# FFN1's last group beside keys and values of blocks 0 to 2, norm products on GpSimd, conditioning columns as dots on VectorE

## What is computed

```python
mod = (silu(c) @ w_ada + b_ada)             # 9 rows of 1024: sh1 sc1 gt1 sh2 sc2 gt2 sh3 sc3 gt3
h = rms_norm(x) * (1 + sc1) + sh1
x = x + 0.5 * gt1 * swiglu(h)               # FFN1, hidden width 2816
h = rms_norm(x) * (1 + sc2) + sh2
x = x + gt2 * (sig(gA) * P_A(chunk band attention) + sig(gB) * P_B(multi-scale pool)) @ w_o
h = rms_norm(x) * (1 + sc3) + sh3
x = x + 0.5 * gt3 * swiglu(h)               # FFN2
```

## Time and profile before

| what | value |
|---|---|
| median of 3 runs | 1545.3 us (1543.4 to 1545.4) |
| the profiled execution | 1544.8 us, its slowest core's span 1543.2 us |
| spans of the 8 cores | 1537.7 to 1543.2 us |
| mean granted TensorE clock | 0.989 to 1.000 |
| bytes moved by DMA on that core | 107.13 MB, mean 69 GB/s |

### The profile page before, as it was taken

How to read it: one execution, slowest core, us unless ns; L and a number is a source line. 1 busy time by engine, 2 the same in 40 slices (tenths; PEclk the granted TensorE clock), 3 DMA queues, 4 the chain that set the end, 5 groups by cost and what they waited for, 6 DMA issues and landing times.

```text
span 1543.2 us, 23259 instructions; the slowest of 8 cores (1537.7 to 1543.2 us)
## 1 busy us (share of the span) xinstructions
PE 1486.7 (96%) x8336; PEld 703.2 (46%) x8336; DVE 815.5 (53%) x1290; ACT 451.3 (29%) x630; POOL 119.4 (8%) x170
## 2 busy tenths in 40 slices
PE   2899999999999999999999999999999999999998
PEld 1344444444444444454564454444444444444443
DVE  2366344172272756678765568746453616162644
ACT  3470111101101036468855453523401010101010
POOL 1100100100001012200000000203000000000000
PEclk9999999999999999999999999999999999999999
DMA  9951433513515211430044363347132221211022
GB/s 204 243 102 28 76 69 55 99 25 69 96 28 102 48 41 38 123 60 15 1 93 86 56 130 63 69 82 116 28 55 53 44 42 16 47 28 28 1 110 109
DMA packets 24303, 107.13 MB, mean 69 GB/s; under 512 B 2816, under 2 KB 3072, under 8 KB 21760
## 3 DMA queue, kind: packets, MB, share of 16 engines
q0 software_dynamic: 21312, 75.67, 29.0%
q1 hardware_dynamic: 2880, 29.98, 5.6%
HBM read 168.71 MB, written 12.58 MB: 117 GB/s over the span
## 4 chain that ended last, share of the span: by engine, by line
PE 91%; DMA 3%; DVE 3%; issue 2%; ACT 1%; POOL 0%; DVEq 0%; ACTq 0%; POOLq 0%
PE ps L714 44%; PE ps L742 21%; PE ps L1081 7%; PE ps L887 4%; PE ps L1113 4%; PE ps L1094 3%; DMA arena<-w_ada 3%; PE ps L1027 2%; DVE arena L513 1%; PE ps L933 1%; PE ps L969 1%; PE ps L870 1%; DVE arena L519 1%; PE ps L563 1%; PE ps L609 1%
## 5 line engine op out<-in xcount | busy, mean ns | idle before, releaser
L714 PE MATMUL ps<-arena 128*128 128x512 bf16 x3152 | 694.4, 381 | 4.4 <-DVE arena L519 4.0
L507 ACT ACTIVATE arena<-ps 128x512 bf16<-128x512 f32 (+3 forms) x426 | 268.5, 652 | 946.3 <-PE ps L714 790.4
L714 PEld LDWEIGHTS ps<-arena 128*128 128x128 bf16 x3152 | 307.8, 98 | 376.3 <-issue 16.2
L519 DVE SCALAR_TENSOR_TENSOR arena<-ps,arena 128x512 f32<-128x512 f32 (+1 forms) x500 | 360.4, 748 | 73.6 <-ACT arena L507 22.6
L513 DVE TENSOR_TENSOR arena<-arena,ps 128x512 bf16<-128x512 bf16 x198 | 135.1, 687 | 486.8 <-PE ps L714 476.1
L742 PE MATMUL ps<-arena 128*128 128x512 bf16 x1584 | 345.0, 379 | 1.3 <-DVE arena L513 1.2
L742 PEld LDWEIGHTS ps<-arena 128*128 128x128 bf16 x1584 | 154.4, 98 | 188.3 <-issue 5.5
L513 DVE TENSOR_TENSOR arena<-arena 128x1024 f32<-128x1024 f32 (+8 forms) x228 | 173.6, 780 | 33.8 <-ACT arena L507 27.6
L1081 PE MATMUL ps<-arena 128*128 128x512 bf16 x512 | 116.3, 379 | 1.4 <-ACT arena L507 1.0
L507 ACT ACTIVATE arena<-arena 128x512 f32<-128x512 f32 (+2 forms) x86 | 89.3, 1053 | 35.2 <-DVE arena L519 20.8
L1081 PEld LDWEIGHTS ps<-arena 128*128 128x128 bf16 x512 | 49.1, 98 | 59.8 <-issue 2.4
(11 more groups left out here) (65 smaller groups left out, 516.6 us busy)
## 6 DMA issues: line engine op xcount, KB each, us to landing
arena<-w_ada POOLq DMA_DIRECT2D x36, 512.0 KB, 8.8
arena<-w_gate POOLq DMA_DIRECT2D x24, 512.0 KB, 8.5
arena<-w1i POOLq DMA_DIRECT2D x22, 512.0 KB, 6.5
arena<-w3i POOLq DMA_DIRECT2D x22, 512.0 KB, 5.3
arena<-x SPq DMA_DIRECT2D x5, 2048.0 KB, 15.5
outT<-arena SPq DMA_DIRECT2D x8, 1024.0 KB, 3.9
arena<-w1o POOLq DMA_DIRECT2D x10, 512.0 KB, 6.8
arena<-w_kqvu POOLq DMA_DIRECT2D x10, 512.0 KB, 7.6
```

The costliest lines, as they stand in the source:

```text
L507: return e.activation(out=o, in_=i, func=func, scale=scale)
L519: return e.scalar_tensor_tensor(out=out, in0=in0() if callable(in0) else in0, scalar=scalar, in1=in1() if callable(in1) else in1, op0=op0, ...
L714: ins = e.matmul(pst(t), lhsT=w[:, kt, :], rhs=hk(b, kt), start=(kt == 0), stop=(kt == 7))
```

## The change

- The last 24 chunks of `w_ada` become 48 dots: `ada_dot` loads 128 rows of the transposed matrix (512 KB, f32, on SyncE's queue) into one of two buffers in `EXPB`'s place and has VectorE multiply them by silu(c) (broadcast to all partitions, `CCB`) with a running sum. They follow three of four units from unit 23 on. A single addition of all 48 biases and the `der` rows come after the last.
- The last group of FFN1 keeps its activations in `ACTL` (block 0 to 2 in the place of the keys of the same block, 3 and 4 in the halo's), the SiLU outputs of blocks 2 to 4 in `SAL`, and its weights in a ring "l" outside of the mixer's slots but one; the group before uses five slots ("p"). Units and outputs of its blocks 2, 3 and 4 get ramps f2, f3 and f4, and all ramps are new. `outp` now has the gate row among the reads of its matrix products.
- The four products of the second and the third norm go to GpSimd; the planner's costs of some operations are changed.
- The bias table comes in four parts into two buffers, not in two into one.
- The last block's stores are split in 4, 2, 1 and 1 tiles, not in 4 and 4.

```diff
@@ -19,11 +19,12 @@
 SILU, EXP, LN, TANH = "silu", "exp", "ln", "tanh"
-RAMPS = {"v0a": (6.86, 12.16), "k0a": (10.15, 11.87), "k0b": (10.76, 11.77), "v0b": (12.6, 12.7),
-         "a0": (10.39, 12.64), "u0": (10.68, 12.89), "k3": (11.4, 12.42), "k4": (11.01, 14.15),
-         "v3": (15.11, 15.16), "v4": (13.29, 13.34), "q4": (13.4, 13.6), "a1": (14.08, 16.3),
-         "g0": (13.99, 15.41), "o0": (17.33, 18.34), "u1": (15.09, 18.95), "g1": (19.52, 20.02),
-         "n1": (16.9, 20.3), "o1": (21.22, 21.31)}
+RAMPS = {"f2": (-2.27, 2.35), "f3": (3.2, 4.57), "f4": (1.96, 11.57), "v0a": (10.79, 16.74),
+         "k0a": (13.06, 13.07), "k0b": (11.58, 11.63), "v0b": (12.47, 16.3), "a0": (3.81, 9.54),
+         "u0": (9.96, 17.67), "k3": (14.97, 15.02), "k4": (11.18, 25.82), "v3": (14.62, 16.19),
+         "v4": (25.19, 33.87), "q4": (11.34, 12.92), "a1": (13.34, 16.32), "g0": (13.27, 15.92),
+         "o0": (9.88, 25.49), "u1": (10.59, 20.44), "g1": (14.47, 25.98), "n1": (18.69, 26.76),
+         "o1": (26.57, 27.85)}
@@ -381,7 +382,9 @@
     cst_d = din("cst", [128, NCST])
-    ada_d = din("w_ada", [36, 128, 2048])
+    ada_d = din("w_ada", [12, 128, 2048])
+    adat_d = din("w_adat", [48, 128, 1024])
+    crow_d = din("crow", [128, 1024])
@@ -450,7 +453,9 @@
     o_w = alloc(6 * 4096)
-    TABT = view(o_mrg, F32, (4 * TABW,))
+    ACTL = [view(o, BF16, (4, TB)) for o in (o_kt, o_kt + 4096, o_kt + 8192, o_mrg, o_mrg + 4096)]
+    SAL = [view(o_mrg + 8192 + 1024 * i, BF16, (TB,)) for i in range(3)]
+    TABT = [view(o, F32, (2 * TABW,)) for o in (o_mrg + 11264, o_x + 2 * 16384 + 8192)]
@@ -475,6 +480,8 @@
              "g": [o_qt, o_qt + 4096, o_expb + 4096, o_att, o_att + 4096] + [o_w + 4096 * i for i in range(6)],
+             "p": [o_w + 4096 * i for i in range(5)],
+             "l": [o_expb, o_expb + 4096, o_att, o_att + 4096, o_qt + 4096, o_w + 5 * 4096],
@@ -533,6 +540,9 @@
         return H[:, b, kt, :]
+    def ramp(t0, t1, n):
+        return lambda i: t0 + (t1 - t0) * (i + 0.5) / n
@@ -584,6 +594,17 @@
+    ADS = [view(o_expb + 4096 * i, F32, (1024,)) for i in range(2)]
+    CCB = view(o_kq, BF16, (1024,))
+
+    def ada_dot(j, deps=()):
+        wt = ADS[j % 2]
+        S.op("sp", lambda e: e.dma_start(out=wt, in_=adat_d[j - 24]), writes=[wt], dma="d_ads%d" % (j % 2), nbytes=1 << 19,
+             deps=deps)
+        S.op("dve", lambda e: e.scalar_tensor_tensor(out=wt, in0=wt, scalar=1.0, in1=CCB, op0=ALU.mult, op1=ALU.mult,
+                                                     accum_out=MOD[:, j:j + 1]),
+             reads=[wt, CCB], writes=[wt, MOD[:, j:j + 1]], cost=1.22)
+
@@ -622,7 +643,10 @@
             rb = bass.AP(rs.tensor, rs.offset, [list(rs.ap[0]), [0, 2], [1, TB]])
-            tt(tb, xp, rb, ALU.mult, [xp, rs], [tb], 1.1)
+            if sub > 0:
+                tt(tb, xp, rb, ALU.mult, [xp, rs], [tb], 2.3, eng="pool")
+            else:
+                tt(tb, xp, rb, ALU.mult, [xp, rs], [tb], 1.22)
@@ -631,7 +655,7 @@
                         out=hk(b, kt), in0=ti, scalar1=s1, scalar2=s2, op0=ALU.mult, op1=ALU.add),
-                        reads=[ti, sc, sh], writes=[hk(b, kt)], cost=0.49)
+                        reads=[ti, sc, sh], writes=[hk(b, kt)], cost=0.6)
@@ -689,11 +713,14 @@
     def ffn(wi_d, wo_dd, sub, blocks, first):
-        ada_next = [12] if first else [36]
+        ada_next = [24] if first else [72]
...
-        def unit(jl, b, wt):
+        def hid(jl, b, last):
+            return ACTL[b][:, jl, :] if last and first else ACTB[:, jl, b, :]
+
+        def unit(jl, b, wt, last=False):
@@ -714,24 +741,29 @@
                     S.op("pe", mm, reads=[wt, H[:, b, :, :]], writes=[t], cost=mmc(8, 512), also=[tb] if t is ta else (), stream="ab")
-            sa = SA[sa_pos[0] % 3]
+            sa = (SAL if last and first and b >= 2 else SA)[sa_pos[0] % 3]
...
             act(sa, lambda: pst(ta), AF.Silu, reads=[ta], writes=[sa], cost=0.6, tset=SILU)
-            tt(ACTB[:, jl, b, :], sa, lambda: pst(tb), ALU.mult, [sa, tb], [ACTB[:, jl, b, :]], 0.69)
+            hd = hid(jl, b, last)
+            tt(hd, sa, lambda: pst(tb), ALU.mult, [sa, tb], [hd], 0.69)
...
             n = ucount[0]
-            if ada_next[0] < 36 and n > 20 and n % 3 == 0:
-                c = ada_next[0]
-                ada_load(c, [uops[max(0, n - 7)]])
-                t = Tile()
-                ada_mm(c, t, c)
-                ada_out(t, c, 1)
+            if ada_next[0] < 72 and n > 22 and n % 4 != 0:
+                j = ada_next[0]
+                if j == 24:
+                    S.op("sp", lambda e: e.dma_start(out=ADS[1], in_=crow_d), writes=[ADS[1]], dma="d_ads1", nbytes=1 << 19,
+                         deps=[uops[10]])
+                    act(CCB, ADS[1], AF.Silu, reads=[ADS[1]], writes=[CCB], cost=1.0, tset=SILU)
+                ada_dot(j, [uops[max(0, n - 4)]])
                 ada_next[0] += 1
-                if ada_next[0] == 36:
+                if ada_next[0] == 72:
+                    lo, hi = 24, 72
+                    tt(MOD[:, lo:hi], MOD[:, lo:hi], CST[:, 8 + lo:8 + hi], ALU.add, [MOD[:, lo:hi], CST], [MOD[:, lo:hi]], 0.17)
...
-        def outp(b, nk, wos):
+        def outp(b, nk, wos, last=False):
+            hd = [hid(jl, b, last) for jl in range(nk)]
@@ -739,10 +771,10 @@
                         c0 = (jl % 2) * 1024 + n * 128
-                        ins = e.matmul(pst(t), lhsT=wos[jl // 2][:, c0:c0 + 128], rhs=ACTB[:, jl, b, :],
+                        ins = e.matmul(pst(t), lhsT=wos[jl // 2][:, c0:c0 + 128], rhs=hd[jl],
...
                     return ins
-                S.op("pe", mm, reads=[w for w in wos] + [ACTB[:, jl, b, :] for jl in range(nk)], writes=[t],
+                S.op("pe", mm, reads=[w for w in wos] + hd + [DER[:, 3 * sub + 2, :]], writes=[t],
@@ -752,7 +784,7 @@
             nk = GSIZES[g]
-            ring = "g" if not first else ("s" if g == 0 else "f")
+            ring = "g" if not first else ("s" if g == 0 else "l" if g == ng - 1 else "p" if g == ng - 2 else "f")
@@ -791,22 +823,27 @@
                             norm(blocks[i + 1], 0)
+                    pf = ramp(*RAMPS["f%d" % b], nk + 2) if lastg and first and b >= 2 else None
                     for jl in range(nk):
-                        unit(jl, b, wts[jl])
+                        if pf:
+                            S.prio = pf(jl)
+                        unit(jl, b, wts[jl], lastg)
                     if lastg:
-                        outp(b, nk, wos)
+                        if pf:
+                            S.prio = pf(nk + 1)
+                        outp(b, nk, wos, lastg)
                         if first:
-                            S.prio = 0.0 if b <= 2 else 9.0
+                            S.prio = 0.0 if b <= 2 else 10.5
...
                         if not first:
-                            for n in range(0, 8, 4):
-                                S.op("sp", lambda e, n=n, b=b: e.dma_start(out=outT[b - 1][:, n:n + 4, :],
-                                                                           in_=XB[:, b - 1, n:n + 4, :]),
-                                     reads=[XB[:, b - 1, n:n + 4, :]], dma="d_st", nbytes=1 << 20,
+                            for n, w in ((0, 4), (4, 2), (6, 1), (7, 1)) if b == blocks[-1] else ((0, 4), (4, 4)):
+                                S.op("sp", lambda e, n=n, w=w, b=b: e.dma_start(out=outT[b - 1][:, n:n + w, :],
+                                                                                in_=XB[:, b - 1, n:n + w, :]),
+                                     reads=[XB[:, b - 1, n:n + w, :]], dma="d_st", nbytes=w << 18,
@@ -841,12 +878,13 @@
     S.prio = 5.0
-    for r in range(2):
-        S.op("sp", lambda e, r=r: e.dma_start(out=TABT, in_=tab_d[r]), writes=[TABT], dma="d_tab",
-             nbytes=128 * 4 * TABW * 4)
-        for h in range(4):
-            src = TABT[:, h * TABW:(h + 1) * TABW]
-            dst = EXPB[:, 4 * r + h, :]
+    for r in range(4):
+        tb_ = TABT[r % 2]
+        S.op("sp", lambda e, r=r, tb_=tb_: e.dma_start(out=tb_, in_=tab_d[r // 2][:, (r % 2) * 2 * TABW:(r % 2 + 1) * 2 * TABW]),
+             writes=[tb_], dma="d_tab%d" % (r % 2), nbytes=128 * 2 * TABW * 4)
+        for h in range(2):
+            src = tb_[:, h * TABW:(h + 1) * TABW]
+            dst = EXPB[:, 2 * r + h, :]
@@ -1238,7 +1273,8 @@
     shared = {
-        "w_ada": np.stack([_cols(w_ada, 256 * cc, 256) for cc in range(36)]),
+        "w_ada": np.stack([_cols(w_ada, 256 * cc, 256) for cc in range(12)]),
+        "w_adat": w_ada.T[3072:].reshape(48, 128, 1024),
@@ -1279,6 +1315,7 @@
         m["cst"] = cst
+        m["crow"] = np.ascontiguousarray(np.broadcast_to(c[b], (128, D)))
...
```

2 lines of the change are left out of this document (removed).

## The result

The changed kernel takes 1550.69 us as the median of five runs (1548.39 to 1553.18), the one before 1544.89 beside it (1542.66 to 1545.4). The ratio is **1.0044, 95% interval 1.0030 to 1.0057**: slower by 6.8 us (4.6 to 8.8), where 13 us of gain were forecast. The profiled execution took 1552.84 us with a span of 1551.3.

A forecast was written before the change was run, and what follows sets the result against it. The prediction took TensorE, busy 96% of the span, as the bound. Its terms, -9.1 + 1.0 - 4 + 0 - 1.1 = -13.2 us against 1544.8, gave 1531.6, stated as 1532 us, range 1524 to 1541.

The forecast's parts named there:

- Part 1: FFN1 after 165 us: 24 conditioning chunks leave TensorE for dots on VectorE, -9.1 us, with +1.0 us of cost.
- +1.0: FFN1's three-step groups: cost of dots slipping into output products and of the gate row wait, between 0 and 3.5 us.
- Part 2: FFN1's last group: keys and values run beside it and fill TensorE's idle time, -4 us, between -14.7 and +18.
- The named stall: 615 to 650 us: TensorE's 2.96 us wait for read-modify-writes behind norm work on VectorE, counted as gone, -3.1 us.
- -1.6 us for the attention's stretch: 650 to 812 us: stretch turns VectorE-bound, but the last block's output products fill in, 7.4 us idle where 9 were.
- The bound of +18: Attention's stretch: worst case for the last group, all eight norm products blocking VectorE for 2.12 us, 27 us idle against 9.
- Part 3: Norms: 36 products go to GpSimd, two blocked scalings per norm, longer chain covered in FFN2, 0 us there (-1 to +3).
- Part 4: Tail: smaller last store of 256 KB, -1.1 us (0 to -1.4); sign: under 3 us from VectorE's end to span's end.
- (d): Rival, attention's stretch: the shared-port lock between GpSimd and VectorE makes the kernel slower, +18, 1553.6 us; chance 0.15.
- (a): Rival, transition: no gain, key and value work only moves and attention idles as much more; 1536 to 1540 us, chance 0.17.
- (c): Rival: TensorE waits among the dots, or for scalar tables beside the keys, 12 us over forecast, 1544 us; chance 0.10.
- (b): Rival, 615 to 981 us: all of TensorE's idle time goes, 1521 us; chance 0.08.

The follow-up runs named there:

- f6: Kernel before, queue orders kept, with only the last 24 conditioning chunks made 48 dots, each alone behind one unit's product: ratio 0.9947.
- f8: Changed kernel, queue orders kept, norm products back on VectorE, each dot straight behind its unit's product, output products not reading the gate row: ratio 0.9989.
- f4: Changed kernel, queue orders kept, with only the 36 norm products moved from GpSimd back to VectorE: ratio 1.0003.
- g1: f8 planned anew with the ramps, priorities and costs of the kernel before, the change's new places kept: ratio 0.9992.
- e4: Kernel before with only the last 24 conditioning chunks made 48 dots on VectorE, all queues planned anew: ratio 1.0029.
- g2: f6 plus the change's split of the last block's stores in 4, 2, 1 and 1 tiles: ratio 0.9944, 1534.49 us.
- f3: Kernel before, queue orders kept, with only the 36 norm products moved to GpSimd at their planned times: ratio 1.0238.
- g3: f3 with the VectorE scalings of the second and third norm moved to ScalarE: ratio 1.0165.
- e1: Changed kernel with the 36 norm products back on VectorE, all queues planned anew: ratio 1.0058.
- e5: Changed kernel without the dots and with the norm products on VectorE, planned anew, so the last group and tail alone: ratio 1.0111.

## Why the prediction was wrong, point by point

The steps from before to the change go over four pairs of kernels, and add up by construction: 1544.9 - 8.2 (dots, f6) + 6.5 (last group and tail, f8) + 2.2 (the dots' planned places and the gate row, f4) + 6.3 (GpSimd products) = 1551.7, which is what the ratio of 1.0044 makes of 1544.9. Only f6 and f8 are on record as of one chip. The steps are differences of ratios and inherit their intervals (f6 alone: 4.9 to 11.4 us of gain); the span medians of the profiled executions give -6.9, +5.8, +2.5 and +5.2. So three steps have a sign clear of noise and a size good to some 2 us; the +2.2 is not clear of noise by the times.

- **Part 1, -9.1 + 1.0.** Right in size if the dots stand where the text put them, one behind a unit: -8.2 measured against -8.1. Wrong for the kernel as planned: -6.0. The +1.0 for dots slipping into the output products is the term that was undersized, +3.1, within its upper bound of 3.5. "Two buffers make at most one dot in some 4 us, against one needed in 4.6" held on average, and the planner's list asked for them in bunches: VectorE waited 62.7 us for loads. The gate row's wait was foreseen as two small instructions, not with the lower clock behind it (0.87 us became 2.3 on the core shown; the lower clock followed on six of eight cores).
- **Part 2, -4.** The step that failed first: +6.5 came in its place, tail included. The named stall did vanish (-2.7 us in the transition). What failed is "It only meets less competition", and the -1.6 us for the attention's stretch, both checked against sums of busy time for each engine (115.5 and 123 us by the rate of 82%). TensorE lost 2.5 us in the last group, 3.7 in keys, values and attention and 2.6 after them, while VectorE was busy for at most 74% of any of these stretches. One wait is traced to its cause: the 2.4 us behind a norm's scaling that GpSimd's sum of squares held up. For the rest the cause is open, and with it whether the places or the plan brought it; the eight norm products in a row are in g1 and e4 and not in f8 or the change. The bound of +18 held it; the best guess had the wrong sign.
- **Part 3, 0.** The second failed step, +6.3. The mis-sized term is the number of blocked scalings, two in each norm: 28 were blocked and not 18, at the 1.6 us each that was taken, 46 us and not 29. So the relief of 1.7 us in each norm was none at all: VectorE gave up 36 products of 1.22 us, 44 us, and its scalings grew by 46. I asked what VectorE's sum would be, and not who stands behind the blocked scaling: the read-modify-writes and evictions that free PSUM, four waits of 1.2 to 2.2 us. FFN2, costed at nothing, lost 0.9 us from the start of its first product to the end of its last (459.8 against 458.9, medians of eight cores).
- **Part 4, -1.1.** Profiles say -0.8 (3.45 against 4.23 us); a store of 256 KB took 3.2 us, not the 2.8 taken. The sign "under 3 us" did not come, and the forecast's own 1.1 us would have left 3.1.
- **The rivals.** (d) named the right engine and the right mechanism for a slower kernel, the lock, but in the attention's products of two SBUF inputs, with VectorE full. The measured densest stretch is at 80%; the loss sits in the norms beside the last group and behind them. (a) is what f8 shows for two of its stretches: 2.7 us gained at the transition, 3.7 given back in the attention's. (c) had the dots' loads and the gate row right. No rival joined the two, each of which alone moves the time less than the gain; together with part 2 they are over it. (b) is out: 24.5 us idle. The sign set for part 2 and rival (d), more than 15 us idle between the last FFN1 unit and the gates, came out at 14.7 (634 to 811 us on the core shown), just short, though part 2 did fail.
- **What stays open.** Where f8's 6 us come from is known by stretch, with one wait of 2.4 us traced. Whether the new places cost anything at all is not shown, since f8 and g1 were both planned with the dots and the queue order of f6 was not. That undoing g1's long wait would gain its 7 us is not shown either: three tries at moving single instructions gained nothing. A split of the eight products into two norms apart in time was not tried, nor was g2 with the new places and a plan made for them. The two thirds of f3's loss that are left in g3 after the scalings went are only argued.

## What to carry to other kernels

Price a move by who stands behind it in the queue of the engine it lands on, which runs in order, and not by the engine's sum of busy time: the same 48 dots were 8.2 us of gain behind units and 14 us of loss two by two. Before moving a product from VectorE to GpSimd, count every VectorE instruction that the two can hold up, and ask whether something that frees PSUM is queued behind one: here the blocked scalings cost VectorE as much as the products had. When a planner makes the order, test parts with the order kept by hand; planned anew, e1, e4 and e5 gave prices of the wrong sign or size. And before blaming a wait on a part, look for the same wait in a run without that part: e4 has g1's.

## What was not expected of the hardware

- A scaling of 0.55 us was held for 4.42 and 5.70 us, beyond the end of one GpSimd instruction into the next. The Trainium skill (page "SBUF — State Buffer", section "Who interferes with whom") has the lock for a whole instruction. The 26 shorter blocks of the change agree with that; in these two rows the waiting VectorE instruction got no turn between two GpSimd instructions.
- A wait of 0.87 us on TensorE was followed by 4 us at a granted clock of 0.57, where the 4.5 us before had 1.00; on another core of the same execution a wait of the same length was followed by a clock of 1.00.
- Each dot with a running sum brings a second instruction of 83 ns on VectorE, 4.0 us for 48, as the group DVE_READ_ACCUMULATOR shows.
